# The second half's causal attentions: first block of queries on its 128 visible keys alone

## What is computed

```python
def sliding_window_attention(q, k, v, sinks):
    ...
    rel = qi - si
    band = (rel >= 0) & (rel < SWA_WINDOW)
    valid = (jnp.arange(n)[:, None, None] * BLOCK + si[None]) >= 0
    mask = band[None] & valid
    scores = jnp.where(mask[None, :, None, None], scores, NEG_INF_2)
    ...

def forgetting_attention(q, k, v, log_f):
    c = jnp.cumsum(log_f, axis=1).transpose(0, 2, 1)
    ...
        logits = jnp.einsum('bqhd,bkhd->bhqk', qi, k).astype(jnp.float32) * scale
        logits = logits + ci[..., :, None] - c[:, :, None, :]
        qpos = i * BLOCK + jnp.arange(BLOCK)
        mask = kpos[None, :] <= qpos[:, None]
        logits = jnp.where(mask, logits, NEG_INF_2)
    ...
```

## Time and profile before

| | |
|---|---|
| median of 3 runs | 2537.09 us (2534.85 to 2544.18) |
| profiled execution, own time | 2547.3 us |
| its span, first to last instruction | 2545.5 us |
| TensorE busy | 2206.9 us (87%), mean granted clock 0.95 |
| VectorE, ScalarE, GpSimd busy | 767.4, 490.2, 186.8 us |
| first causal attention | about 1787 to 1868 us (layer 0), 2179 to 2261 us (layer 1) |
| second causal attention | 1869 to 1969 us and 2262 to 2361 us |

### The profile page before, as it was taken

The page is one execution under the profiler, slowest core; times in us unless marked ns, Lnnn a source line. Parts: engine busy times, 40 slices in busy tenths (PEclk is TensorE's granted clock), DMA queues, the critical chain, the costliest instruction groups (busy, mean ns, idle before and its releaser), DMA issues.

```text
span 2545.5 us, 30929 instructions
## 1 busy us (share of the span) xinstructions
PE 2206.9 (87%) x12339; PEld 1315.5 (52%) x12340; DVE 767.4 (30%) x1770; ACT 490.2 (19%) x1061; POOL 186.8 (7%) x234
## 2 busy tenths in 40 slices
PE   5999996877878889987888778779999999999998
PEld 3556565333443434656434433335775575776565
DVE  0344554111111006446111111114444413445413
ACT  1142202111111112311211111111212222111222
POOL 1000001111110110001011111110000000000000
PEclk8999998999999989998899999999999999999999
DMA  9233746999999884476899999995212242321231
GB/s 349 79 143 149 299 157 243 415 425 419 417 416 379 309 351 145 174 286 228 347 385 382 412 399 425 413 413 213 102 72 100 100 161 108 129 100 72 103 128 46
DMA packets 61793, 635.94 MB, mean 250 GB/s; under 512 B 15500, under 2 KB 15764, under 8 KB 23936
## 3 DMA queue, kind: packets, MB, share of 16 engines
q1 hardware_dynamic: 41584, 588.39, 57.4%
q0 software_dynamic: 19248, 39.92, 4.7%
q10 hardware_dynamic: 864, 6.29, 0.6%
HBM read 617.68 MB, written 44.09 MB: 260 GB/s over the span
## 4 chain that ended last, share of the span: by engine, by line
PE 70%; DMA 18%; DVE 5%; issue 3%; ACT 3%; SPq 0%; POOL 0%; ACTq 0%; POOLq 0%; DVEq 0%
PE ps L791 18%; DMA ring<-in_moe 13%; PE ps L906 9%; PE ps L489 8%; PE ps L920 6%; PE ps L1027 4%; PE ps L477 3%; PE ps L633 3%; PE ps L511 2%; PE ps L797 2%; PE ps L1099 2%; PE ps L706 2%; PE ps L520 2%; DMA ring<-in_denseA 2%; DVE scr L1639 2%
## 5 line engine op out<-in xcount | busy, mean ns | idle before, releaser
L791 PE MATMUL ps<-ring,scr 128*64 128x256 f32 (+1 forms) x4800 | 708.2, 454 | 121.7 <-issue 79.6
L791 PEld LDWEIGHTS ps<-ring,scr 128*64 128x64 f32 x4800 | 354.9, 146 | 454.1 <-issue 283.5
L906 PE MATMUL ps<-ring,hT 128*128 128x512 f32 (+1 forms) x576 | 245.2, 578 | 5.8 <-ACT hT L1547 5.8
L1639 DVE TENSOR_TENSOR scr<-ps,scr 128x512 f32<-128x512 f32 (+3 forms) x98 | 54.7, 558 | 591.4 <-PE ps L791 464.6
L489 PE MATMUL ps<-ring,hT 128*128 128x512 f32 (+1 forms) x512 | 204.1, 560 | 8.3 <-ACT hT L1409 7.2
L1310 POOL DMA_INDIRECT ys_scratch<-scr,ytab x128 | 124.9, 976 | 915.7 <-DVE scr L2258 840.7
L2258 DVE COPY scr<-ps 128x1024 f32<-128x1024 f32 x64 | 78.4, 1225 | 375.7 <-PE ps L791 339.1
L1366 ACT ACTIVATE scr<-ps 128x256 f32<-128x256 f32 (+1 forms) x168 | 74.8, 457 | 532.1 <-PE ps L477 532.0
L906 PEld LDWEIGHTS ps<-ring,hT 128*128 128x128 f32 x576 | 108.7, 193 | 117.1 <-issue 106.9
L1499 ACT ACTIVATE scr<-ps 128x512 f32<-128x512 f32 x64 | 38.2, 597 | 626.5 <-PE ps L791 571.0
L489 PEld LDWEIGHTS ps<-ring,hT 128*128 128x128 f32 x512 | 100.5, 198 | 105.8 <-issue 93.6
(11 more groups left out here) (320 smaller groups left out, 2260.8 us busy)
## 6 DMA issues: line engine op xcount, KB each, us to landing
ring<-in_moe SPq DMA_DIRECT2D x192, 2048.0 KB, 10.2
ring<-in_denseB SPq DMA_DIRECT2D x48, 2048.0 KB, 7.8
ring<-in_denseA SPq DMA_DIRECT2D x36, 2048.0 KB, 13.9
scr<-ys_scratch POOLq DMA_DIRECT2D x6, 1024.0 KB, 7.0
modB<-mod_scratch POOLq DMA_DIRECT2D x10, 512.0 KB, 12.2
ring<-kv_scratch SPq DMA_DIRECT2D x2, 2048.0 KB, 8.1
tok_scratch<-hb POOLq DMA_DIRECT2D x6, 512.0 KB, 2.9
memT_scratch<-modB ACTq DMA_DIRECT2D x2, 1024.0 KB, 5.3
```

What stands on the lines that cost most here:

```text
L791: last = mm(out, lhs(c)[:, 0:64], w(c)[:, half * q:half * (q + 1)], start=(c == 0), stop=(c == n - 1))
L906: last = mm(T["open"][:, 0:cols], hT16[:, c, t * P:(t + 1) * P], w[:, c, 0:cols], start=(c == 0), stop=(c == DC - 1))
L1639: return V.tensor_tensor(out, a, b, op)
```

## The change

For n = 0 the scores, the mask, the maximum, the exponential, the transposes and the product with the values take 128 keys; for n = 1 nothing changes. In the second attention L983 is left out for n = 0. The number of keys in `attention` of VectorE may now be 128, hence the new condition there; the first half and the memory attention issue what they did.

```diff
@@ TensorE @@
             attention([(n, h) for n in range(NX) for h in range(NH)],
-                      gqa_score(qaT, kaT, lambda n: 0, lambda n: 256),
-                      lambda n, h, k: vaB[:, k, (h // GQA) * HD:(h // GQA + 1) * HD], lambda n: 2, HD, fill)
+                      gqa_score(qaT, kaT, lambda n: 0, lambda n: (n + 1) * P),
+                      lambda n, h, k: vaB[:, k, (h // GQA) * HD:(h // GQA + 1) * HD], lambda n: n + 1, HD, fill)
...
             def fox_score(n, h):
                 bank = sc_bank()
                 o = HD * (h % 2)
-                mm(bank[:, 0:256], qbT[o:o + HD, h // 2, n * P:(n + 1) * P], kbT[o:o + HD, h // 2, :],
+                w = (n + 1) * P
+                mm(bank[:, 0:w], qbT[o:o + HD, h // 2, n * P:(n + 1) * P], kbT[o:o + HD, h // 2, 0:w],
                    start=True, stop=False)
-                mm(bank[:, 0:256], spf[:, 0, h:h + 1].to_broadcast([P, P]), const("uincl", 256),
-                   start=False, stop=False)
-                mm(bank[:, 0:256], spf[:, 1, h:h + 1].to_broadcast([P, P]), const("z0", 256),
-                   start=False, stop=True).then_inc(sc_full, 1)
+                last = mm(bank[:, 0:w], spf[:, 0, h:h + 1].to_broadcast([P, P]), const("uincl", w),
+                          start=False, stop=(n == 0))
+                if n > 0:
+                    last = mm(bank[:, 0:w], spf[:, 1, h:h + 1].to_broadcast([P, P]), const("z0", w),
+                              start=False, stop=True)
+                last.then_inc(sc_full, 1)
...
             attention([(n, h) for n in range(NX) for h in range(NH)], fox_score,
-                      lambda n, h, k: vbB[:, k, h * HD:(h + 1) * HD], lambda n: 2, HD, decay_and_fill)
+                      lambda n, h, k: vbB[:, k, h * HD:(h + 1) * HD], lambda n: n + 1, HD, decay_and_fill)
@@ ScalarE @@
-            attention([(n, h) for n in range(NX) for h in range(NH)], lambda n: 2, True, NH, softplus_exps)
-            attention([(n, h) for n in range(NX) for h in range(NH)], lambda n: 2, False, NH, decay_exps)
+            attention([(n, h) for n in range(NX) for h in range(NH)], lambda n: n + 1, True, NH, softplus_exps)
+            attention([(n, h) for n in range(NX) for h in range(NH)], lambda n: n + 1, False, NH, decay_exps)
@@ VectorE @@
-                elif nk == 256:
-                    tell(tt(s, bank[:, 0:256], m, ALU.add), sc_free)
+                elif nk <= 256:
+                    tell(tt(s, bank[:, 0:nk], m, ALU.add), sc_free)
...
-            attention([(n, h) for n in range(NX) for h in range(NH)], lambda n: 256,
-                      lambda n: const("causal", 256) if n == 0 else const("gt", 256),
+            attention([(n, h) for n in range(NX) for h in range(NH)], lambda n: (n + 1) * P,
+                      lambda n: const("causal") if n == 0 else const("gt", 256),
                       None, True, NH, HD, put_a, beside_a)
...
-            attention([(n, h) for n in range(NX) for h in range(NH)], lambda n: 256,
-                      lambda n: const("causal", 256) if n == 0 else const("z1", 256),
+            attention([(n, h) for n in range(NX) for h in range(NH)], lambda n: (n + 1) * P,
+                      lambda n: const("causal") if n == 0 else const("z1", 256),
                       lambda n, h: cs[:, 64 + 8 * n + h:65 + 8 * n + h], False, NH, HD, put_b, beside_b)
```

## The result

Over 15 runs of each, the changed kernel takes 2523.25 us (median; 2507.24 to 2533.38) and the kernel before 2543.24 us (2533.14 to 2556.42). The ratio is 0.9916, 95% interval 0.9894 to 0.9939: 15 to 27 us faster. The sign came as forecast, and the median lies 12 us above the forecast and above the range that was given.

A forecast was written before the change was run, and what follows sets the result against it. TensorE was taken to set the pace in the causal attentions. Savings of 4.37 us (first) and 8.68 (second) per layer, 26.1 for two layers, taken from 2537.1 gave 2511.0 us; range 2504 to 2520.

The forecast's parts named there:

- The terms of the sum: Savings per n = 0 unit: product 0.225 us, transpose 0.105, scores 0.21 in the first attention, 0.85 in the second.
- fifth rival: Removed transposes and products in both attentions save their full printed lengths: 30.6 us saved, 2506.5 us; chance 0.03.
- The starts: Where each attention begins, the first transpose comes earlier: 0.47 us in the first, 0.94 in the second.
- The short groups: Shorter matmul groups in n = 0 units expose waits and don't pay in full: 2 to 6 us lost; chance 0.14.
- another pace: VectorE or ScalarE sets the pace of the n = 0 units and nothing is saved: 2537 us; chance 0.04.
- The clock: TensorE's clock also falls at the second attention's start, through added idle time: 3.4 to 4.8 us lost; chance 0.07.
- Slower: The clock stays low through a whole stretch of eight n = 0 units, costing 35 us: 2546 us; chance 0.02.

The follow-up runs named there:

- sums_four: The kernel before with the cumulative-sum matmuls of dt issued four times over, 24 more small matmuls over two layers; 772.8 us from first attention to end, against 758.7.
- early_both: early_decay plus a half stream piece issued ahead of the first attention's first transpose, none at its last unit; ratio to the kernel before 0.9900.
- sums_both: sums_decay joined with early_both's half stream piece ahead of the first attention's first transpose, the sums one unit earlier; ratio to the kernel before 0.9859.
- sums_moved: sums_decay without the early decay, so the first decay is back behind the first transpose; ratio to the kernel before 0.9922.
- early_decay: The changed kernel with the first decay's four matmuls issued ahead of the second attention's first transpose; ratios to the kernel before 0.9889 and 0.9894.
- first_only: The kernel before with the change in the first causal attention alone; ratio to the kernel before 0.9977.
- sums_decay: early_decay with the cumulative sums issued before unit 14's piece of the first attention, VectorE's stream piece 8 after the first scores; ratio to the kernel before 0.9913.

## Why the prediction was right or wrong

*The terms of the sum* held. Product 0.22 us (0.225 taken), transpose 0.11 (0.105), 128 score columns 0.21 (0.21), the second attention's scores 0.85 (0.85); the dense parts 3.61 and 6.83 us against 3.59 and 6.79. The wide units of the first half were the right rows to read them from. The 0.2 us beside a 64-row score stayed, as taken (0.41 for 128 columns). The Trainium skill ("TensorE: Matmul & The Clock Gate", "Part 4: PE-mode transpose") has about 275 ns for a 128 x 128 transpose in a kernel, in bf16. For the float32 ones here that would have been too much: the one removed was worth 0.11. The fifth rival, printed lengths, fails by the same distances: product and transpose were worth 0.33 us together and not 0.47.

*The starts.* The second attention's first transpose came 1.07 us earlier (0.94 taken, with nothing for ScalarE, whose exponential took 0.40 instead of 0.51), after a wait of 0.88 (0.9). The first attention's came 0.59 earlier (0.47) after 1.57 us; I had written 1.9. With these the sum without the clock is 26.6 to 26.8 us.

*The short groups* (first rival) and *another pace* (third) did not appear: no idle row stands between units.

*The clock* (second rival) is what went wrong; the sum has nothing for it. It cost 5.5 us: 4.0 at the new place, where the clock fell in both layers and where the rival had said 3.4 to 4.8, and 1.5 at the old one, where it stayed low for longer, which the rival had not counted. Its mechanism, the wait, fits layer 0; in layer 1 the fall came ahead of the wait. I gave it 0.07. The step that failed is the argument against it: that at the memory attention's start TensorE is busy 2.25 of 4 us with the clock at 1.00, and would be busy over 3 of 4 here. A busy share was the wrong thing to compare. sums_four is busy 10.00 of 10.00 us and the clock falls. And the two places differ in what stands in front and between. In the kernel before, timeline of TensorE:

```profile
2087.73 6.53 PE L1099 MATMUL ps<-hT,ring 128*128 128x128 f32 x57
2095.50 1.99 PE L1116 MATMUL ps<-ring,scr 128*128 128x256 f32 x8 [1.24 <-DVE small L2524]
2098.55 0.44 PE L477 MATMUL ps<-cst,scr 128*128 128x128 f32 x2 [1.06 <-ACT scr L1379]
```

The memory attention starts behind a long run of 128-column matmuls, with 256-column ones between its two waits. At the changed place I had counted the idle time and overlooked the seven tiny matmuls in front of it, and I had thinned the scores between the two. That these matter is shown by early_both, whose clock falls in both layers, and sums_both, which keeps it without them. The Trainium skill (same page, "Why this matters for your kernels") says that idle gaps between bursts of matmuls bring the clock down. sums_moved agrees in direction, with a gap of 1.67 us and no tiny matmuls; the page speaks of longer gaps than any here, and by the measurement shorter ones are enough behind thin work.

*The range* failed for a second reason. The prediction took 2537.1 us as the level of the kernel before and 3 us as the scatter of a median. Over 15 runs that level is 2543.2, and its single runs lie over a range of 23 us. 2523.2 is 12.2 above the forecast: 6.1 are the level and 6.1 the smaller saving (20.0 between the medians). Either alone would have left 2517, inside the range. The level was the luck of a small sample: 2537.1 is the median of the first three of these fifteen runs. The profiled execution and the median of three stood 10 us apart in the material before, and that should have been read as scatter.

*Slower* (fourth rival): the low clock was left within one unit each time, so 5.5 us were lost and not 26.

## What to carry to other kernels

Work taken from a saturated in-order engine came off at the distances between starts, to 0.04 us per dense part, read from the same lines at another width. Look then at the places where the engine starts up again: thin work, waits and tiny matmuls stand together there, and the clock took back a fifth of the gain. Real work moved into such a gap gained the gap and, both times, the clock behind it (early_decay), but the gap that it left elsewhere took part of it back (early_both).

## What the runs showed of the hardware

- TensorE's granted clock fell to 0.50 without any idle time, in a run of matmuls of 8 and 16 columns followed by 256-column ones (sums_four, both layers; first_only, one layer), and cost 4.4 us each time.
- The same ingredients in other amounts: 1.6 us of tiny matmuls and narrow scores with no wait yet, no fall in four layers of early_decay and a fall in two of the changed kernel. Narrow scores, a decay and a 0.54 us wait, no tiny ones: none in two (sums_decay), and none in two with another 0.47 us of wait ahead of the scores (sums_both). Narrow scores and 1.67 us of wait: a fall in both (sums_moved). 0.47 us of wait, then 1.6 us of tiny matmuls, then narrow scores: a fall in both (early_both).
- Each further transpose of 128 x 128 float32 in a stretch costs 0.11 us start to start (one 0.21, two 0.32, four 0.53), and a score matmul of 128 columns is 0.21 us cheaper than one of 256.
- One unchanged stage of about 530 us, with the DMA engines at 95 to 97%, differed by 9.6 us between two looks at the same kernel.
